# The prompt's attention weighing as three products of high and low parts, in one unit with score and look

## The chip, the cores and the metric

The kernel runs on one core of a Trainium2 chip as a single launch. The metric is device time in microseconds (us), the median of three runs. TensorE (PE in the rows) multiplies matrices, with its weight loads shown apart as PEld; VectorE (DVE), ScalarE (ACT) and GpSimd (POOL) do the elementwise work; SyncE (SP) and GpSimd issue the DMAs. Every engine takes its own instructions strictly in the order in which the program lists them and waits on counters (semaphores) where it needs another engine's result.

## What is computed, cut to what matters

The kernel is one inference step of a two-layer decoder for a prompt of 2048 tokens and for 8 sample sequences of 8 tokens. Layer 0 has eight heads of "FoX" attention (attention with a forget gate), whose prompt part and sample part are the subject here; retention, a gated linear recurrence, projections and norms around it are not touched.

```python
def fox_prompt(q, k, v, logf):                 # per head: 2048 queries, 2048 keys, 64 values wide
    cum = jnp.cumsum(logf, axis=1)
    ...
    s = jnp.einsum('bqhd,bkhd->bhqk', qi, k) * scale
    s = s + ci.transpose(0, 2, 1)[..., None] - cum_t[:, :, None, :]
    s = jnp.where((qpos[:, None] >= kpos[None, :])[None, None], s, NEG_INF)
    p = jax.nn.softmax(s, axis=-1)
    return jnp.einsum('bhqk,bkhd->bqhd', p.astype(v.dtype), v)      # the weighing

def fox_sample(q, k, v, logf, k_past, v_past, logf_past):           # 8 x 8192 cached rows, in pages of 128
    ...
```

All of it is float32.

## The kernel before

The program runs in stages one after the other, each a function with its own loops: input projections, a small preparation, `attention`, `retention`, and the second layer. Only `attention` is touched.

`attention` does two jobs at a time: for head `t` of the prompt the whole causal attention, and for one sample batch the attention over its 64 cached pages (of the next batch the score part, of this batch the weighing part). A loop runs over eight heads, two heads to an iteration, the last two peeled; before it stands an `opening` for the first head's turned inputs and the first batch's scores.

**The prompt's work in one head** is 40 steps. Queries lie in four groups of 512 columns (`G`), keys in tiles of 128, and group `g` needs the key tiles 0 to 4g+3: 4 + 8 + 12 + 16 = 40 steps `s`. The last four tiles of each group are on the diagonal and narrower: 512, 384, 256 and 128 columns. A step has these parts:

- *score* (`score`, L1567 and L1568): two matmuls into one of two PSUM banks `ps_k[s % 2]`. On the diagonal VectorE adds a mask (L1402).
- *exp* (L1288): ScalarE writes `prob[s % 4]`, plain float32.
- *weigh* (L1583): one float32 matmul, stationary `v` with a column of ones (65 columns), moving `prob`, added up in `ps_o`. The program issues one matmul; the trace shows each as two records.
- *look* (L1549, L1550): the scores of a step 18 places ahead (`AHEAD`), turned round, into the one bank `ps_n`; VectorE takes the row maximum (L1383; on the diagonal it first adds a mask, L1379). These give each query's maximum before its scores are made.

A group ends with *keep* (ScalarE copies `ps_o`) and *out* (turned back and normed). During steps 8 to 15 the next head's queries and keys are turned (`turn`): transposes into `ps_x`, ScalarE takes the high part, VectorE the low part, GpSimd a copy (L1242, L1244).

**The samples' work in one head** is 16 rounds of four *page turns* (`s_turn`, L1629: four 128x128 transposes into the one bank `ps_t`, which ScalarE empties for even pages, L1319, and VectorE for odd pages, L1434), a *page score* (L1637, L1641) and a *page weighing* (L1668), and in every other round a *flip* (`s_flip`, L1651: four transposes of sample probabilities into the same bank `ps_t`, emptied by VectorE, L1443; behind it VectorE takes a maximum, L1438). A page turn has to wait until the page before it has been copied out of `ps_t`.

**What sets the order.** `fox_events` lists the prompt's events of a head with a cost each, `samp_events` the samples', and `merge` interleaves the two lists: it takes the next event of whichever list is less far through its total cost, and keeps events of the same kind at least `SPACE` = 0.85 apart where it can. The merged list is walked by every engine: each emits, in that order, its own part of each event. So the list sets TensorE's order and VectorE's and ScalarE's as well. An event of cost 0 is emitted where the merge comes to it, which may be after sample events. Before the change a step gave two events with a cost, score and look together, and the weighing of two steps earlier.

## Time and profile before

| | us |
|---|---|
| median of three runs | 3978.82 (3969.96 to 3981.21) |
| the profiled execution, its own time | 3970.3 |
| its span in the trace | 3968.7 |
| attention's opening (first page turn to the first score) | 925 to 1063 |
| attention's eight heads | 1063 to 2268 |

The page gives TensorE 88% of the span as busy, VectorE 41%, ScalarE 34%, GpSimd 11%. The granted TensorE clock is 0.943 of full speed over the span. The rows further down come from four views: the windows view (busy time of each engine in a stretch, with the granted clock), the lines view (groups of like instructions), the waits view (who waited for whom), and the timeline (instructions in order of time). A timeline row is: start, duration, engine, line, operation, tiles written and read, shapes, how many were merged, and in brackets the idle time before it with what ended it. A matmul's recorded duration runs past the start of the next one, since they are pipelined; what it costs in a stream is the distance from its start to the next start.

### The profile page before, as it was taken

To read this page: it belongs to the slowest core of one execution; us is meant where nothing else is said; L and a number is where in the kernel's file an instruction comes from. 1 tells how busy PE (TensorE), PEld (TensorE's weight loads), DVE (VectorE), ACT (ScalarE), POOL (GpSimd) and SP (SyncE) were. 2 spreads that over 40 slices of the span, in tenths; PEclk is the share of its full clock that TensorE was granted. 3 is DMA by queue.
4 is the path that set the end of the run, shared out by engine and by line. 5 is a ranking of instruction groups with operands and counts; after the bars stand their busy time and mean duration, and the time that the engine had idled before them with its cause. 6 is when DMAs were issued, how large, how long until landed. Compare 5 with 4: busy or idle time off the path is not lost. (4 is left out here: it accounts for less than half of the span.)

```text
span 3968.7 us, 65033 instructions
## 1 busy us (share of the span) xinstructions
PE 3509.9 (88%) x21092; PEld 2631.3 (66%) x21092; DVE 1636.0 (41%) x3074; ACT 1347.8 (34%) x2380; POOL 446.6 (11%) x683
## 2 busy tenths in 40 slices
PE   6999699975799999989999776999968999769998
PEld 5888588863455565555555465788856767558887
DVE  3222311323344454444444255433335676643333
ACT  3111211101233333333333243333335666632322
POOL 0000000101022222222222244000000000000000
PEclk9999899976799999999999988999989999879999
DMA  5223532435577777777776587333234333142221
GB/s 156 108 107 132 170 105 96 141 89 152 152 228 233 224 232 232 236 222 234 231 231 202 153 290 253 130 130 129 105 136 165 126 123 123 58 168 90 90 90 55
DMA packets 381102, 627.46 MB, mean 158 GB/s; under 512 B 124121, under 2 KB 182401, under 8 KB 380802
## 3 DMA queue, kind: packets, MB, share of 16 engines
q1 hardware_dynamic: 339026, 487.55, 37.8%
q0 software_dynamic: 41792, 136.48, 10.8%
q8 instruction: 135, 2.21, 0.2%
q14 instruction: 149, 1.22, 0.1%
HBM read 488.67 MB, written 135.22 MB: 157 GB/s over the span
## 5 line engine op out<-in xcount | busy, mean ns | idle before, releaser
L1629 PEld LDWEIGHTS att_samp_ps_t<-att_ident,att_samp_k_ring 128*128 128x128 f32 x2048 | 238.7, 147 | 283.1 <-issue 233.6
L1629 PE MATMUL att_samp_ps_t<-att_ident,att_samp_k_ring 128*128 128x128 f32 x2048 | 339.7, 291 | 84.9 <-DVE att_samp_kt L1434 43.8
L123 PE MATMUL in_ps_z<-in_w_hi,in_u_hi 128*128 128x512 f32 x952 | 376.3, 395 | 40.8 <-DVE in_w_lo L157 40.8
L1229 POOL DMA_DIRECT2D att_samp_v_ring<-cache_v x512 | 274.9, 537 | 974.4 <-issue 971.1
L124 PE MATMUL in_ps_z<-in_w_lo,in_u_hi 128*128 128x512 f32 x952 | 374.6, 394 | 0.0
L125 PE MATMUL in_ps_z<-in_w_hi,in_u_lo 128*128 128x512 f32 x952 | 374.6, 393 | 0.0
L1319 ACT COPY att_samp_kt<-att_samp_ps_t 128x512 f32<-128x512 f32 x256 | 149.8, 585 | 502.8 <-PE att_samp_ps_t L1629 501.5
L1434 DVE COPY att_samp_kt<-att_samp_ps_t 128x512 f32<-128x512 f32 x256 | 176.2, 688 | 293.6 <-PE att_samp_ps_t L1629 288.5
L1583 PE MATMUL att_fox_ps_o<-att_fox_prob,att_fox_v_one 128*65 128x512 f32 (+3 forms) x640 | 287.7, 533 | 3.8 <-ACT att_fox_prob L1288 3.8
L1383 DVE TENSOR_REDUCE att_fox_part_max<-att_fox_ps_n 128x1 f32<-128x512 f32 (+2 forms) x320 | 195.0, 609 | 123.1 <-PE att_fox_ps_n L1550 112.9
L123 PEld LDWEIGHTS in_ps_z<-in_w_hi,in_u_hi 128*128 128x128 f32 x952 | 181.4, 191 | 80.1 <-issue 28.6
L1288 ACT ACTIVATE att_fox_prob<-att_fox_ps_k 128x512 f32<-128x512 f32 (+1 forms) x320 | 169.9, 536 | 183.5 <-DVE att_fox_ps_k L1402 103.2
L123 PE MATMUL tail_ps_g<-tail_wg_hi,tail_h_hi 128*128 128x512 f32 x544 | 216.1, 397 | 13.2 <-DVE tail_p_lo L2317 9.9
L125 PE MATMUL tail_ps_g<-tail_wg_hi,tail_h_lo 128*128 128x512 f32 x544 | 212.6, 391 | 0.0
L124 PE MATMUL tail_ps_g<-tail_wg_lo,tail_h_hi 128*128 128x512 f32 x544 | 212.5, 391 | 0.0
L125 PEld LDWEIGHTS in_ps_z<-in_w_hi,in_u_lo 128*128 128x128 f32 x952 | 181.3, 190 | 38.3
L124 PEld LDWEIGHTS in_ps_z<-in_w_lo,in_u_hi 128*128 128x128 f32 x952 | 181.5, 191 | 37.3
L1668 PEld LDWEIGHTS att_samp_ps_v<-att_samp_v_ring,att_samp_prob_t 128*32 128x32 f32 x4096 | 115.5, 111 | 82.8 <-issue 69.1
L2345 DVE SCALAR_TENSOR_TENSOR tail_e<-tail_ps_g,tail_e 128x512 f32<-128x512 f32 x68 | 47.0, 691 | 277.9 <-ACT tail_ps_g L2278 277.9
L1567 PE MATMUL att_fox_ps_k<-att_fox_q_a,att_fox_k_a 128*128 128x512 f32 (+1 forms) x320 | 160.4, 501 | 0.0
L1641 PE MATMUL att_samp_ps_s<-att_samp_kt,att_samp_q_diagonal 128*32 128x512 f32 x1024 | 145.7, 643 | 3.5 <-DVE att_samp_kt L1434 3.5
L1668 PE MATMUL att_samp_ps_v<-att_samp_v_ring,att_samp_prob_t 128*32 128x128 f32 x4096 | 137.7, 276 | 10.4 <-DMA att_samp_v_ring<-cache_v 9.9
(376 smaller groups left out, 7006.4 us busy)
## 6 DMA issues: line engine op xcount, KB each, us to landing
att_samp_v_ring<-cache_v POOLq DMA_DIRECT2D x512, 256.0 KB, 3.8
att_samp_k_ring<-cache_k SPq DMA_DIRECT2D x512, 256.0 KB, 3.6
tail_a_hi<-a_hi SPq DMA_DIRECT2D x34, 512.0 KB, 5.7
tail_a_lo<-a_lo SPq DMA_DIRECT2D x34, 512.0 KB, 5.9
in_w_stage<-w_in_even SPq DMA_DIRECT2D x64, 256.0 KB, 6.4
lru_u_hi<-u_hi SPq DMA_DIRECT2D x8, 2048.0 KB, 8.0
lru_u_lo<-u_lo SPq DMA_DIRECT2D x8, 2048.0 KB, 13.1
in_x<-x SPq DMA_DIRECT2D x17, 512.0 KB, 3.8
```

Source lines behind the costliest of these rows:

```text
L123: pe.matmul(out, act_hi, w_hi, start=start, stop=False)
L124: pe.matmul(out, act_hi, w_lo, start=False, stop=False)
L125: return pe.matmul(out, act_lo, w_hi, start=False, stop=stop)
L1229: pool.dma_start(v_ring[:, p, g, :], row(io["cache_v"], page)).then_inc(vp_in[y], 16)
L1288: act.activation(prob[:, s % 4, r:G], ps_k[:, s % 2, r:G], ACT.Exp).then_inc(exped.sem, 1)
L1319: act.copy(kt[:, n % 2, :, p * PAGE:(p + 1) * PAGE], ps_t[:, :].rearrange("p (a k) -> p a k", a=PAIRS)).then_inc(k_even.sem, 1)
L1383: dve.tensor_reduce(part_max[:, g, b % B4, c:c + 1], ps_n[:, 0:w], AX.X, ALU.max).then_inc(maxed.sem, 1)
L1434: dve.tensor_copy(kt[:, n % 2, :, p * PAGE:(p + 1) * PAGE], ps_t[:, :].rearrange("p (a k) -> p a k", a=PAIRS)).then_inc(k_odd.sem, 1)
L1567: pe.matmul(ps_k[:, s % 2, r:G], k_a[:, par, k], q_a[:, par, q], start=True, stop=False)
L1583: pe.matmul(ps_o[0:HD + 1, r:G], v[:, par, kt, :], prob[:, s % 4, r:G], start=kt == 0, stop=kt == B4 * (g + 1) - 1).then_inc(weighed.sem, 1)
L1629: last = pe.transpose(ps_t[:, a * PAGE:(a + 1) * PAGE], k_ring[:, n % 2, p, a * P:(a + 1) * P], ident[:, :])
L1668: last = pe.matmul(ps_v[strip, g, :], prob_t[:, c % 2, at:at + 2 * R], v_ring[:, p, g, a * P:(a + 1) * P], start=c == 0 and p == 0, stop=c ...
```

## The change

The weighing becomes three matmuls in the reduced float32 type (`F32R`) that scores and looks use: values and probabilities are each split into a high part (rounded to `F32R`) and a low part (the rest), and `split3` (unchanged, L119 to L125) adds up high x high, low x high and high x low. For that:

- ScalarE takes the exponential twice from the same score bank, into `p_hi` (`F32R`, 3 buffers) and into `prob` (float32, 2 buffers instead of 4).
- VectorE gets a new event *cut*: `p_lo = prob - p_hi`. The weighing waits for it (`prob_cut`) instead of for the exponential.
- The values of a head are no longer loaded by `fetch` straight into place. A new event *load_v* loads them into the buffer of the turned queries once those are turned (SyncE), and *cut_v* makes `v_hi` (ScalarE) and `v_lo` (VectorE). They are 66 columns wide instead of 65.
- In the merge's list, weighing of step s-2, score of s and look make one event with the summed cost (0.7 + 0.46 + 0.46). The *cut* of step s-1 follows it as an event of cost 0.

```diff
@@ fox_events
-            for s in range(steps + 2):
+            for s in range(steps + LAG):
+                unit, cost = [], 0.0
+                if s >= LAG:
+                    g, kt = group_of(s - LAG)
+                    unit.append(("weigh", g, s - LAG, kt))
+                    cost += 0.7 * cut_width(kt - B4 * g)
                 if s < steps:
                     g, kt = group_of(s)
-                    pair = [("score", g, s, kt)]
-                    cost = 0.46 * cut_width(kt - B4 * g)
+                    unit.append(("score", g, s, kt))
+                    cost += 0.46 * cut_width(kt - B4 * g)
...
-                        pair.append(("look", dt, ng, b, c, n))
+                        unit.append(("look", dt, ng, b, c, n))
                         cost += 0.46
-                    out.append((cost, *pair))
-                if s >= 2:
-                    g, kt = group_of(s - 2)
-                    out.append((0.87 * cut_width(kt - B4 * g), ("weigh", g, s - 2, kt)))
+                out.append((cost, *unit))
+                if 1 <= s <= steps:
+                    out.append((0.0, ("cut", group_of(s - 1)[0], s - 1, group_of(s - 1)[1])))
...
+                    if not last and s == TURN + 2 * GQ + 2:
+                        out.append((0.0, ("load_v", 1)))
+                    if not last and s == TURN + 2 * GQ + 7:
+                        out.append((0.0, ("cut_v", 1)))
@@ sync
-                sp.dma_start(v[:, par, :, 0:HD], io["fv"]...).then_inc(v_in[par], 16)
...
+            def load_v(t, i, par, dt):
+                t, i, par = ahead(t, i, par, dt)
+                sp.wait_ge(*turned.at(t))
+                sp.sem_inc(sp_passed, 1)
+                sp.dma_start(nat[:, 0], io["fv"][0:PT, :, bass.ds(t * HD, HD)]...).then_inc(v_in[par], 16)
@@ scalar
-                act.wait_ge(*(weighed.at(t, s - 4) if s >= 4 else weighed.at(t - 1, s - 4 + steps)))
-                act.activation(prob[:, s % 4, r:G], ps_k[:, s % 2, r:G], ACT.Exp).then_inc(exped.sem, 1)
+                act.wait_ge(*(weighed.at(t, s - 3) if s >= 3 else weighed.at(t - 1, s - 3 + steps)))
+                act.activation(p_hi[:, s % 3, r:G], ps_k[:, s % 2, r:G], ACT.Exp)
+                act.wait_ge(*(prob_cut.at(t, s - 2) if s >= 2 else prob_cut.at(t - 1, s - 2 + steps)))
+                act.activation(prob[:, s % 2, r:G], ps_k[:, s % 2, r:G], ACT.Exp).then_inc(exped.sem, 1)
+
+            def cut_v(t, i, par, dt):
...
+                act.copy(v_hi[:, par, :, 0:HD], nat[:, 0]).then_inc(v_high.sem, 1)
@@ vector
+            def cut(t, i, par, g, s, kt):
+                r = max(kt - B4 * g, 0) * P
+                dve.wait_ge(*exped.at(t, s))
+                dve.wait_ge(*(weighed.at(t, s - 2) if s >= 2 else weighed.at(t - 1, s - 2 + steps)))
+                dve.tensor_tensor(p_lo[:, s % 2, r:G], prob[:, s % 2, r:G], p_hi[:, s % 3, r:G].bitcast(F32), ALU.subtract)\
+                    .then_inc(prob_cut.sem, 1)
+
+            def cut_v(t, i, par, dt):
...
+                dve.tensor_tensor(v_lo[:, par, :, 0:HD], nat[:, 0], v_hi[:, par, :, 0:HD].bitcast(F32), ALU.subtract).then_inc(v_low.sem, 1)
@@ tensor
-                pe.wait_ge(*exped.at(t, s))
+                pe.wait_ge(*prob_cut.at(t, s))
...
-                pe.matmul(ps_o[0:HD + 1, r:G], v[:, par, kt, :], prob[:, s % 4, r:G],
-                          start=kt == 0, stop=kt == B4 * (g + 1) - 1).then_inc(weighed.sem, 1)
+                split3(pe, ps_o[0:HD + 2, r:G], v_hi[:, par, kt, :], v_lo[:, par, kt, :], p_hi[:, s % 3, r:G], p_lo[:, s % 2, r:G],
+                       kt == 0, kt == B4 * (g + 1) - 1).then_inc(weighed.sem, 1)
```

How the order moves is shown at two places of a head. The first is the stretch behind score and look of step 8, where a round's page score and page weighing stand. TensorE before (`ps_n` is the look, `ps_t` a page turn, `ps_s` the page score, `ps_v` the page weighing, `ps_o` the prompt's weighing, `ps_x<-ident,fox_natural` a turn of the next head's inputs):

```order
L1550 MATMUL att_fox_ps_n<-att_fox_k_b,att_fox_q_b 128x512
L1629 MATMUL att_samp_ps_t<-att_ident,att_samp_k_ring 128x128 x4
L1641 MATMUL att_samp_ps_s<-att_samp_kt,att_samp_q_diagonal 32x512 x4
L1663 ISA
L1668 MATMUL att_samp_ps_v<-att_samp_v_ring,att_samp_prob_t 32x128 x16
L1627 REGISTER_ALU
L1629 MATMUL att_samp_ps_t<-att_ident,att_samp_k_ring 128x128 x4
L1583 MATMUL att_fox_ps_o<-att_fox_prob,att_fox_v_one 65x512
L1629 MATMUL att_samp_ps_t<-att_ident,att_samp_k_ring 128x128 x4
```

TensorE after, at the same place:

```order
L1599 MATMUL att_fox_ps_n<-att_fox_k_b,att_fox_q_b 128x512
L1678 MATMUL att_samp_ps_t<-att_ident,att_samp_k_ring 128x128 x4
L1690 MATMUL att_samp_ps_s<-att_samp_kt,att_samp_q_diagonal 32x512 x4
L1712 ISA
L1717 MATMUL att_samp_ps_v<-att_samp_v_ring,att_samp_prob_t 32x128 x16
L1676 REGISTER_ALU
L1678 MATMUL att_samp_ps_t<-att_ident,att_samp_k_ring 128x128 x4
L1644 REGISTER_ALU
L1646 ISA
L1649 MATMUL att_fox_ps_x<-att_ident,att_fox_natural 64x128 x4
L1628 REGISTER_ALU
L123 MATMUL att_fox_ps_o<-att_fox_p_hi,att_fox_v_hi 66x512
```

The weighing no longer parts two page turns; it has moved behind the turn of the next head's inputs, to the front of the next unit. VectorE at this place, before (score mask, look maximum, odd page's copy, low part of the turned inputs):

```order
L1402 TENSOR_TENSOR att_fox_ps_k<-att_fox_ps_k,att_mask_t 128x128
L1377 REGISTER_ALU
L1383 TENSOR_REDUCE att_fox_part_max<-att_fox_ps_n 128x1
L1431 REGISTER_ALU
L1434 COPY att_samp_kt<-att_samp_ps_t 128x4x128
L1420 REGISTER_ALU
L1423 TENSOR_TENSOR att_fox_q_a<-att_fox_ps_x,att_fox_q_a 64x512
```

and after:

```order
L1439 TENSOR_TENSOR att_fox_ps_k<-att_fox_ps_k,att_mask_t 128x128
L1414 REGISTER_ALU
L1420 TENSOR_REDUCE att_fox_part_max<-att_fox_ps_n 128x1
L1480 REGISTER_ALU
L1483 COPY att_samp_kt<-att_samp_ps_t 128x4x128
L1443 REGISTER_ALU
L1445 TENSOR_TENSOR att_fox_p_lo<-att_fox_prob,att_fox_p_hi 128x512
L1469 REGISTER_ALU
L1472 TENSOR_TENSOR att_fox_q_a<-att_fox_ps_x,att_fox_q_a 64x512
```

The cut for the next weighing (`p_lo`) stands behind the look's maximum and behind the copy of the odd page, whose transposes TensorE issues last before that weighing. The second place is a flip, four steps later. VectorE after:

```order
L1420 TENSOR_REDUCE att_fox_part_max<-att_fox_ps_n 128x1
L1490 REGISTER_ALU
L1491 REGISTER_ALU
L1492 COPY att_samp_prob_t<-att_samp_ps_t 128x512
L1487 TENSOR_REDUCE att_samp_tops<-att_samp_scores 128x1
L1443 REGISTER_ALU
L1445 TENSOR_TENSOR att_fox_p_lo<-att_fox_prob,att_fox_p_hi 128x128
```

Here the copy of the flip and the samples' maximum (`tops`) stand ahead of the cut as well; before, the same two were followed by no work that a weighing waits for.

## Rows read from the trace of the kernel before

**Rows 1.** Windows: stretch, each engine's busy us (instructions), granted clock, DMA share, GB/s.
```profile
1227.00:1386.00 159.00, 144.28 (x1259) 90.48 (x1258) 75.86 (x167) 58.81 (x125) 39.73 (x73) 0.99 0.75 232
...
2018.00:2173.50 155.50, 145.29 (x1259) 91.64 (x1259) 75.37 (x165) 57.41 (x119) 39.74 (x73) 0.99 0.71 220
2173.50:2268.00 94.50, 83.30 (x787) 50.71 (x784) 31.36 (x79) 29.37 (x61) 30.05 (x56) 0.98 0.56 162
```

**Rows 2.** Waits, 1060 to 2270: who waited for whom, us in total, times, longest.
```profile
PE att_fox_ps_o L1583 <- ACT att_fox_prob L1288: 3.8, 7, 0.6
```

**Rows 3.** Timeline, 1500 to 1503: TensorE's steps at full width.
```profile
1500.81 1.02 PE L1583 MATMUL att_fox_ps_o<-att_fox_prob,att_fox_v_one 128*65 128x512 f32 x2
...
1501.72 0.66 PE L1629 MATMUL att_samp_ps_t<-att_ident,att_samp_k_ring 128*128 128x128 f32 x4
...
1502.13 0.48 PE L1567 MATMUL att_fox_ps_k<-att_fox_q_a,att_fox_k_a 128*128 128x512 f32 x1
...
1502.45 0.40 PE L1568 MATMUL att_fox_ps_k<-att_fox_q_b,att_fox_k_b 98*128 98x512 f32 x1
...
1502.69 0.40 PE L1549 MATMUL att_fox_ps_n<-att_fox_k_a,att_fox_q_a 128*128 128x512 f32 x1
...
1502.92 0.39 PE L1550 MATMUL att_fox_ps_n<-att_fox_k_b,att_fox_q_b 96*128 96x512 f32 x1
```

**Rows 4.** Timeline, 1503 to 1507: look's maximum; page, page score, page weighing, odd page.
```profile
1503.34 0.63 PE L1629 MATMUL att_samp_ps_t<-att_ident,att_samp_k_ring 128*128 128x128 f32 x4
1503.35 0.69 DVE L1383 TENSOR_REDUCE att_fox_part_max<-att_fox_ps_n 128x1 f32<-128x512 f32 x1 [0.15 <-PE att_fox_ps_n L1550]
...
1503.90 1.07 PE L1641 MATMUL att_samp_ps_s<-att_samp_kt,att_samp_q_diagonal 128*32 128x512 f32 x8
...
1504.78 1.06 PE L1668 MATMUL att_samp_ps_v<-att_samp_v_ring,att_samp_prob_t 128*32 128x128 f32 x32
...
1505.77 0.66 PE L1629 MATMUL att_samp_ps_t<-att_ident,att_samp_k_ring 128*128 128x128 f32 x4
...
...
1506.46 0.69 DVE L1434 COPY att_samp_kt<-att_samp_ps_t 128x512 f32<-128x512 f32 x1 [2.42 <-PE att_samp_ps_t L1629]
```

**Rows 5.** Timeline, 1508 to 1511: an odd page right behind a masked look.
```profile
1508.61 0.65 PE L1629 MATMUL att_samp_ps_t<-att_ident,att_samp_k_ring 128*128 128x128 f32 x4
1508.78 0.30 DVE L1379 TENSOR_TENSOR att_fox_ps_n<-att_fox_ps_n,att_mask 128x128 f32<-128x128 f32 x1 [1.63 <-PE att_fox_ps_n L1550]
...
1509.12 0.56 DVE L1383 TENSOR_REDUCE att_fox_part_max<-att_fox_ps_n 128x1 f32<-128x384 f32 x1
1509.59 0.68 DVE L1434 COPY att_samp_kt<-att_samp_ps_t 128x512 f32<-128x512 f32 x1
...
1510.42 0.63 PE L1629 MATMUL att_samp_ps_t<-att_ident,att_samp_k_ring 128*128 128x128 f32 x4 [0.30 <-DVE att_samp_kt L1434]
```

**Rows 6.** Lines, 1060 to 2270: busy us, mean ns of one.
```profile
L1438 DVE TENSOR_REDUCE att_samp_tops<-att_samp_scores 128x1 f32<-128x512 f32 x58 | 39.3, 677 | 3.2 <-ACT att_samp_scores L1325 2.2 <-DVE att_fox_q_a L1423 0.6
...
L1288 ACT ACTIVATE att_fox_prob<-att_fox_ps_k 128x512 f32<-128x512 f32 x224 | 134.4, 601 | 90.8 <-PE att_fox_ps_k L1568 80.1 <-DVE att_fox_ps_k L1402 10.6
...
L1244 POOL CAST att_fox_k_a<-att_fox_k_a 64x512 fp32r<-64x512 f32 x28 | 17.1, 609 | 17.3 <-ACT att_fox_k_a L1299 15.9 <-issue 0.9 <-POOL att_fox_q_b L1242 0.2
```

**Rows 7.** One line's instructions: duration in ns, min/median/max; high-low split elsewhere.
```profile
L157 DVE TENSOR_TENSOR in_w_lo<-in_w_stage,in_w_hi x56: 681/692/695, 17.1 to 484.2; 128x512 fp32r<-128x512 f32 x56
```

**Rows 8.** Timeline: the end of a head on TensorE.
```profile
1382.12 0.43 PE L1590 MATMUL att_fox_ps_x<-att_ident,att_fox_o_t 65*128 65x65 f32 x4 [1.57 <-ACT att_fox_o_t L1293]
1385.88 0.47 PE L1629 MATMUL att_samp_ps_t<-att_ident,att_samp_k_ring 128*128 128x128 f32 x1 [3.32 <-issue]
```

**Rows 9.** Windows in which TensorE is less busy: granted clock behind POOL's busy time.
```profile
1382.00:1390.00 8.00, 4.11 (x16) 3.11 (x16) 1.93 (x6) 3.07 (x11) 0.00 (x0) 0.57 0.71 143
...
970.00:985.00 15.00, 10.31 (x67) 5.77 (x65) 7.44 (x16) 3.51 (x6) 0.00 (x0) 1.00 0.51 167
1015.00:1060.00 45.00, 32.41 (x135) 15.23 (x135) 8.10 (x12) 8.19 (x14) 0.00 (x0) 0.61 0.43 133
```

More of the change, by code:

```diff
@@ L963, in attention @@
         AHEAD = 18
+        LAG = 2
         TURN = 8
@@ L1058, in attention @@
         weighed = ph.count("weighed", steps, 4)
+        prob_cut = ph.count("prob_cut", steps, 4)
+        sp_passed = ph.sem("sp_passed")
+        v_high = ph.count("v_high")
+        v_low = ph.count("v_low")
         o_copied = ph.count("o_copied", GQ)
@@ L1195, in s_score @@
                     load_bias(b + 1, n // 2 + 2 - NVC)
-            one, step = run({"s_turn": s_turn, "s_score": s_score})
+            def load_v(t, i, par, dt):
+                t, i, par = ahead(t, i, par, dt)
+                sp.wait_ge(*turned.at(t))
+                sp.sem_inc(sp_passed, 1)
+                sp.dma_start(nat[:, 0], io["fv"][0:PT, :, bass.ds(t * HD, HD)].rearrange("t p d -> p t d")).then_inc(v_in[par], 16)
+            one, step = run({"load_v": load_v, "s_turn": s_turn, "s_score": s_score})
             one(-1, -1, 1, opening)
             sp.wait_ge(*turned.at(0))
+            sp.wait_ge(*v_low.at(0))
             fetch(1, 1)
@@ L1348, in s_share @@
                 act.activation(share[:, :], moved[:, :, 0], ACT.Exp, bias=least[:, :], scale=-1.0).then_inc(shared.sem, 1)
-            one, step = run({"top": top_keep, "exp": exps, "keep": copy_out, "turn": turn, "s_place": s_place, "s_turn": s_turn,
+            one, step = run({"top": top_keep, "exp": exps, "cut_v": cut_v, "keep": copy_out, "turn": turn, "s_place": s_place, "s_turn": s_turn,
                              "s_keep": s_keep, "s_exp": s_exp, "s_exp_new": s_exp_new, "s_share": s_share})
@@ L1510, in s_rows @@
                     .then_inc(out_kept.sem, 1)
-            one, step = run({"look": look, "make_top": make_top, "score": mask_score, "out": norm, "turn": turn, "s_turn": s_turn, "s_top": s_top,
+            one, step = run({"look": look, "cut": cut, "cut_v": cut_v, "make_top": make_top, "score": mask_score, "out": norm, "turn": turn, "s_turn": s_turn, "s_top": s_top,
                              "s_flip": s_flip, "s_bias_new": s_bias_new, "s_negate": s_negate, "s_flip_new": s_flip_new, "s_total": s_total,
```

28 lines of the change are left out of this document (21 added, 7 removed).

## The prediction

> **What bounds the kernel now.** Read the windows first [rows 1]. From 1227 to 2173.5 lie six equal heads, so one takes 157.8 us, and TensorE is busy for 144 to 146 us of it at a granted clock of 0.99. VectorE is busy for 75 and ScalarE for 57 to 59. So TensorE is the bound of the heads, and the weighing, which the change shortens, lies on it. Then the waits [rows 2]: today's weighing hardly ever waits for its exponential, 3.8 us in all. That is what the change touches, since it puts one more engine between exponential and weighing. Last the timeline [rows 3 to 5], which shows what each step costs in the stream and how long VectorE needs from a look, or from a page, until TensorE can go on. The waits of the six heads are short but many; which wait ends last has to be read step by step.
>
> **What the change saves on TensorE.** A full weighing starts at 1500.81 and the page behind it at 1501.72: 0.91 us. A matmul of the reduced type costs 0.24 from start to start (1502.45 to 1502.69, 1502.69 to 1502.92) [rows 3]; I take 0.23, and three are 0.69. Gain 0.22. Of 320 weighings 224 are full, and they give 49 us. The narrower ones I put at zero: the new cost there has three matmuls' fixed parts in it and the old one is plainly proportional to columns. The price of 0.23 comes from matmuls with 128 stationary columns; with 66 there is no reason in the rows for another.
>
> **What it adds off TensorE.** A second exponential per step, 0.60 [rows 6], on ScalarE; a subtraction with two operands in SBUF per step on VectorE, 0.69 for 512 columns by a like one elsewhere [rows 7]; per head a copy and a subtraction of 1024 columns, twice that row at most. VectorE goes from 75 to about 100 us per head and ScalarE from 58 to about 80, so neither becomes the bound by its load. The load of the values moves in SyncE's queue behind the turn of the queries, which lies three steps back by then; behind it queue the page loads, and I cost that at nothing, since there is nothing left to wait for. If it did wait, page turns would wait too.
>
> **What it adds as a chain.** TensorE's order of one step is now weigh, score, look as one unit, then sample work, then the next unit, which begins with a weighing. That weighing needs its cut; VectorE does the cut behind the maximum of the look that TensorE has just issued, and, where the merge has put a page's or a flip's copy ahead of it, behind that too. TensorE stands at the weighing, with score, look and every later page queued behind it. I count from the point at which TensorE could start its next work after a look, 0.24 after the start of the look's second matmul, and price how late the weighing starts. I went through the 38 units of a head in the order, four cases:
>
> - A, cut right behind the look's maximum (12 units). From 1502.92 + 0.24 = 1503.16: the maximum runs to 1504.04 [rows 4], the cut 0.69 more, and some 0.15 pass from VectorE's end to TensorE's start (1510.27 to 1510.42) [rows 5]: 1.72 after the point. A masked look adds up to 0.3, so 1.8 each, 22 us. TensorE has one or two pages to do there, which fit inside.
> - B, an odd page or a flip between. In rows 5 the point is the page's start, 1508.61; mask, maximum and page copy end at 1510.27, 1.66 later; cut and hand-over add 0.84: 2.5. Four such with an odd page, two of them lengthened by work on the next head's inputs: 11 us. Seven flips, six with the samples' maximum (0.68, [rows 6]) ahead of the cut as well: 3.1 each, 22 us.
> - C, page, page score, page weighing, odd page, then the cut (9 units). In rows 4 that odd page starts 2.6 after the point (1505.77) and its copy ends at 1507.15, 4.0 after; the cut 0.69 and 0.15: 4.8, 43 us. Today the weighing starts 0.5 after that page's start.
> - D, cut early, but an odd page and then a whole round follow (4 units). The second page waits for the copy of the first, 1.8 (1508.61 to 1510.42, [rows 5]); the round from page to odd page adds 2.4 (1503.34 to 1505.77, [rows 4]) and that page 0.4: 4.6 each, 18 us.
>
> The last two units of a head, with the samples' closing arithmetic on VectorE, I put at 10 us. That makes 126 us between units. The units: 0.69 + 0.56 (score: 0.32 + 0.24) + 0.47 (look) = 1.72 at full width [rows 3], 60 us for the 38, the narrower ones scaled by their columns. The first two steps of a head take 4, and its end 2 (two weighings and the wait of 1.57 for the last copy, [rows 8]). Sum: 192 us, against 157.8: **34 us more per head**, and 239 for seven. The eighth head has no page turns: its 20 units with a look cost 1.7 + 1.8, and the 18 without, where only exponentials (1.2), cut and hand-overs lie between a score and its weighing two units on, about 1.8 each; with start and end 108 against 94.5 [rows 1], 14 more. Together 253 us with TensorE's clock as it is now.
>
> **The clock.** The sum has TensorE idle for some 68 of 192 us per head, in pieces of one to two and a half us. What the clock does then is shown only elsewhere. Around the waits at a head's end, 1.57 and 3.32 [rows 8], the granted clock is 0.57 over 8 us, so partly at the lower of the two levels (1.2 GHz against 2.4). From 1015 to 1060 TensorE is busy for 72% and is granted 0.61; from 970 to 985 it is busy for 69% and is granted 1.00 [rows 9]. The new heads would be busy for about 70%, in the same region, with denser work than those stretches. I take a mean of 0.9, nearer the full clock because every round still holds a long unbroken run. TensorE's work is then 124 us a head and some 80 in the last, 950 us in all; at 0.9 it takes 106 more.
>
> Sum: 253 + 106 = 359 us on the profiled execution's 3970.3, so 4329. The median of the runs lies 8.5 above that execution, so **4335 us**, 9% more.
>
> **A rule on the shared port.** The heads' VectorE instructions of today that I priced read PSUM or one SBUF tensor, so no row shows the cut beside GpSimd's casts of 0.61 [rows 6], eight a head. The Trainium skill, SBUF — State Buffer, section "SBUF: two separate sides", says that a VectorE operation with two SBUF inputs and a GpSimd operation that reads SBUF lock each other out for the whole instruction, whoever starts first. No run here shows it yet. By that rule each cast could hold up a cut by its whole length: by an estimate from the row, at most 8 x 0.61 x 8 = 39 us more; by the rows alone, nothing. I leave it out of the sum.
>
> **Rivals.** (1) *Chain, but no loss of clock*: the pieces of idle time are too short to matter, as from 970 to 985. 3979 + 253 = 4232. (2) *Chain, and a deeper loss*: at a mean of 0.75 TensorE's 950 us take 317 more: 4549. The rows from 1015 to 1060 speak for it, the denser work against. (3) *Chain half hidden*: VectorE takes the cuts earlier than I think, or today's head holds waits that go away; 17 a head, 3979 + 126 = 4105, and in the mildest form no change. (4) *Faster*: the cut is off TensorE's path. This is decided behind a look: if the cut ended before the pages that stand there (0.4 to 0.7 in A, 2.9 in C), the weighing would start as today and only the 49 us would count, 3930. For it speaks that today's weighing waits for nothing [rows 2]; against it, that the chain of 1.7 or more begins with the look itself, and its parts are rows of their own: the maximum in rows 4, the cut in rows 7, the hand-over in rows 5. (5) *The three products don't run at 0.23* with 66 stationary columns but at twice that: 0.69 x 224 = 155 more, about 4490. Nothing in the rows speaks for it.
>
> **How the numbers follow.** Forecast 0.43; rival (1) 0.22; (2) 0.13; (3) 0.11, a third of it without change; (4) 0.08; (5) 0.03. A measurement of this kernel tells 0.3%, about 12 us, from no change. So faster 0.08, the same 0.04, slower 0.88. The range goes from 4110 (chain mostly half hidden) to 4530 (clock at about 0.76 with the chain); below it are (4) and most of (3), above it half of (2).
>
> **What would show it.** In the profile after, the first of the weighing's three matmuls (line 123, `att_fox_ps_o`) should be the costliest waiter on TensorE, ended by VectorE's `att_fox_p_lo`, with some 300 us over the phase where 3.8 stand now; a full weighing should cost 0.69 from start to start; heads should last 190 to 210 us; page turns' own waits should fall. Granted clock in the heads should be 0.85 to 0.95. A head of 157 us or less, or a weighing that still waits for nothing, would make the prediction wrong at the chain; a head of 192 with the clock at 0.99 would make it wrong at the clock alone.

## The result, and the profile after

The changed kernel takes **4253.6 us** (median of 4 runs, 4249.6 to 4262.8) beside 3975.4 of the kernel before: ratio 1.0716, 95% interval 1.0699 to 1.0733 (the two medians alone give 1.0700). It is 278 us slower. The profiled execution has a span of 4251.3 us, 282.6 above that of before (3968.7). TensorE's first work of each head shows where they lie: the heads now begin at 1059.0, 1254.6, 1448.5, 1639.9, 1834.2, 2025.6, 2216.1 and 2408.1, and the last ends at 2543.3. Seven heads took 1110.3 us and take 1349.1, so 238.8 more; the last took 94.5 and takes 135.2, 40.7 more; the opening is 4 shorter, and what follows the attention 7 longer.

First the windows of one middle head, of its last microseconds, and of the last head in two pieces (columns as in [rows 1]).

```profile
1448.50:1639.90 191.40, 146.79 (x1300) 102.77 (x1301) 98.10 (x204) 75.03 (x157) 40.80 (x73) 0.95 0.63 190
1624.00:1634.60 10.60, 7.91 (x84) 4.73 (x82) 5.77 (x15) 2.68 (x8) 3.75 (x7) 1.00 0.77 265
1634.60:1648.30 13.70, 9.21 (x46) 7.49 (x50) 6.74 (x20) 6.13 (x19) 0.00 (x0) 0.50 0.63 139
1648.30:1743.80 95.50, 72.69 (x660) 51.19 (x652) 51.77 (x106) 38.67 (x83) 23.11 (x40) 1.00 0.62 186
2408.10:2491.00 82.90, 60.37 (x644) 43.48 (x647) 28.37 (x62) 21.85 (x51) 30.04 (x56) 0.79 0.64 185
2491.00:2543.30 52.30, 36.59 (x185) 21.91 (x185) 24.70 (x58) 24.32 (x51) 0.00 (x0) 0.96 0.00 1
```

The head lasts 191.4 us and TensorE is busy for 146.8 of them; before, it was 144 to 146 of 157.8. VectorE and ScalarE have risen to 98 and 75 (forecast about 100 and 80) and bound nothing by their load. The granted clock is 0.95: full for most of a head, and at the lower level around its end. In the last head no engine but these three works behind 2491: the sample work is used up there.

Then TensorE's waits over the eight heads (who waited for whom, us in total, times, longest), which answer to [rows 2]. First those of the page turns in the kernel before:

```profile
PE att_samp_ps_t L1629 <- DVE att_samp_kt L1434: 26.4, 35, 1.9
PE att_samp_ps_t L1629 <- ACT att_samp_kt L1319: 6.6, 9, 2.5
PE att_samp_ps_t L1629 <- DVE att_samp_prob_t L1443: 4.6, 15, 0.4
```

and in the changed kernel:

```profile
PE att_fox_ps_o L123 <- DVE att_fox_p_lo L1445: 194.4, 179, 3.3
PE att_samp_ps_t L1678 <- ACT att_samp_kt L1355: 45.4, 64, 2.5
PE att_samp_ps_t L1678 <- DVE att_samp_kt L1483: 29.7, 29, 1.3
PE att_samp_ps_t L1678 <- DVE att_samp_prob_t L1492: 28.1, 28, 1.2
PE att_samp_ps_v L1717 <- DMA att_samp_v_ring<-cache_v: 19.6, 9, 3.5
```

The 3.8 us of before have become 194 us in which the weighing waits for the cut. But page turns wait, too, 103 us over these heads where it was 38, and the experiments show that this is a cost of its own.

Two stretches of the timeline, to be held against [rows 4, 5]. First one of case C, a look with page, page score, page weighing and odd page behind it:

```profile
1710.68 0.61 ACT L1316 ACTIVATE att_fox_prob<-att_fox_ps_k 128x512 f32<-128x512 f32 x1
...
1712.18 0.34 PE L1599 MATMUL att_fox_ps_n<-att_fox_k_b,att_fox_q_b 96*128 96x384 f32 x1
1712.36 0.60 PE L1678 MATMUL att_samp_ps_t<-att_ident,att_samp_k_ring 128*128 128x128 f32 x4
...
1712.89 0.56 DVE L1420 TENSOR_REDUCE att_fox_part_max<-att_fox_ps_n 128x1 f32<-128x384 f32 x1
...
1715.19 0.66 PE L1678 MATMUL att_samp_ps_t<-att_ident,att_samp_k_ring 128*128 128x128 f32 x4
1715.88 0.69 DVE L1483 COPY att_samp_kt<-att_samp_ps_t 128x512 f32<-128x512 f32 x1 [2.44 <-PE att_samp_ps_t L1678]
1716.49 0.68 DVE L1445 TENSOR_TENSOR att_fox_p_lo<-att_fox_prob,att_fox_p_hi 128x512 fp32r<-128x512 f32 x1
...
1717.23 0.45 PE L123 MATMUL att_fox_ps_o<-att_fox_p_hi,att_fox_v_hi 128*66 128x512 f32 x1 [1.38 <-DVE att_fox_p_lo L1445]
```

VectorE stands idle for 2.44 us ahead of the page's copy, with the next cut behind that copy; the cut's own input, the exponential in the first row, was ready at 1711.29, 5.2 us before the cut began. The weighing starts 2.0 us after the page and waits 1.38 for the cut. Now case A, with two pages behind the look:

```profile
1708.83 0.40 PE L1599 MATMUL att_fox_ps_n<-att_fox_k_b,att_fox_q_b 96*128 96x512 f32 x1
...
1709.07 0.60 PE L1678 MATMUL att_samp_ps_t<-att_ident,att_samp_k_ring 128*128 128x128 f32 x4
1709.27 0.69 DVE L1420 TENSOR_REDUCE att_fox_part_max<-att_fox_ps_n 128x1 f32<-128x512 f32 x1 [0.33 <-PE att_fox_ps_n L1599]
...
1709.71 0.58 ACT L1355 COPY att_samp_kt<-att_samp_ps_t 128x512 f32<-128x512 f32 x1 [1.49 <-PE att_samp_ps_t L1678]
1709.88 0.68 DVE L1445 TENSOR_TENSOR att_fox_p_lo<-att_fox_prob,att_fox_p_hi 128x512 fp32r<-128x512 f32 x1
1709.90 1.13 POOL L1270 CAST att_fox_k_a<-att_fox_k_a 64x512 fp32r<-64x512 f32 x1
...
1710.35 0.66 PE L1678 MATMUL att_samp_ps_t<-att_ident,att_samp_k_ring 128*128 128x128 f32 x4 [0.68 <-ACT att_samp_kt L1355]
...
1710.76 0.48 PE L123 MATMUL att_fox_ps_o<-att_fox_p_hi,att_fox_v_hi 128*66 128x512 f32 x1
```

Maximum, cut and hand-over end where I had put them, 1.69 us after 1709.07. Yet the weighing waits for nothing: the second page started only at 1710.35, since it writes the PSUM bank of the first and had to wait 0.68 for that one's copy. Two causes end here at the same time, and only a run without the cut can tell which of them sets it.

### The profile page after: what moved, and what is told of

Read it like the earlier page. It is cut to its first block and busy times, and to the rows that moved or that the text cites. A ratio compares the mean times of both kernels' runs of the same rounds, so it can differ in the third digit from the quotient of the medians.

```text
span 4251.3 us, 67158 instructions
## 1 busy us (share of the span) xinstructions
PE 3530.4 (83%) x21412; PEld 2722.3 (64%) x21412; DVE 1822.4 (43%) x3403; ACT 1495.5 (35%) x2708; POOL 452.6 (11%) x683
## 5 line engine op out<-in xcount | busy, mean ns | idle before, releaser
L1678 PEld LDWEIGHTS att_samp_ps_t<-att_ident,att_samp_k_ring 128*128 128x128 f32 x2048 | 248.3, 149 | 251.8 <-issue 179.0
L125 PE MATMUL in_ps_z<-in_w_hi,in_u_lo 128*128 128x512 f32 x952 | 372.9, 392 | 0.0
L123 PE MATMUL att_fox_ps_o<-att_fox_p_hi,att_fox_v_hi 128*66 128x512 f32 (+1 forms) x320 | 139.4, 436 | 200.4 <-DVE att_fox_p_lo L1445 194.4
L1314 ACT ACTIVATE att_fox_p_hi<-att_fox_ps_k 128x512 fp32r<-128x512 f32 (+1 forms) x320 | 171.5, 536 | 299.2 <-PE att_fox_ps_k L1617 163.0
L123 PEld LDWEIGHTS att_fox_ps_o<-att_fox_p_hi,att_fox_v_hi 128*66 128x66 f32 x320 | 45.5, 142 | 268.6 <-DVE att_fox_p_lo L1445 255.1
L125 PE MATMUL tail_ps_g<-tail_wg_hi,tail_h_lo 128*128 128x512 f32 x544 | 213.3, 392 | 0.0
L125 PEld LDWEIGHTS in_ps_z<-in_w_hi,in_u_lo 128*128 128x128 f32 x952 | 180.3, 189 | 38.1
L1445 DVE TENSOR_TENSOR att_fox_p_lo<-att_fox_prob,att_fox_p_hi 128x512 fp32r<-128x512 f32 (+1 forms) x320 | 192.2, 603 | 12.7 <-ACT att_fox_prob L1316 11.0
```

What stands on the lines that cost most here:

```text
L123: pe.matmul(out, act_hi, w_hi, start=start, stop=False)
L125: return pe.matmul(out, act_lo, w_hi, start=False, stop=stop)
L1314: act.activation(p_hi[:, s % 3, r:G], ps_k[:, s % 2, r:G], ACT.Exp)
L1445: dve.tensor_tensor(p_lo[:, s % 2, r:G], prob[:, s % 2, r:G], p_hi[:, s % 3, r:G].bitcast(F32), ALU.subtract)\
L1678: last = pe.transpose(ps_t[:, a * PAGE:(a + 1) * PAGE], k_ring[:, n % 2, p, a * P:(a + 1) * P], ident[:, :])
```

## The experiments

The theory at the start was the chain through VectorE; the rival, that the unit itself costs the time; a third, that the new arithmetic does, whatever the order. Medians are beside the kernel before on the same chip (3970 to 3975), each ratio with its 95% interval. "Late" is, as in the prediction, the start of a weighing after the point 0.24 behind the start of the look's second matmul, a mean over six heads.

**The cut ahead of the maximum.** TensorE's order is untouched.

```diff
                 unit, cost = [], 0.0
+                if 1 <= s <= steps:
+                    unit.append(("cut", group_of(s - 1)[0], s - 1, group_of(s - 1)[1]))
                 if s >= LAG:
...
                 out.append((cost, *unit))
-                if 1 <= s <= steps:
-                    out.append((0.0, ("cut", group_of(s - 1)[0], s - 1, group_of(s - 1)[1])))
```

> The changed kernel with one event moved: the cut of step s-1 stands ahead of the unit of step s, so on VectorE ahead of the look's maximum and of the page and flip copies behind it; TensorE's own order is the same. Theory (chain look, maximum, cut, weighing): the waits of the weighing for the low part, 194 us in the changed kernel, fall below 30; heads fall from 192 to about 160; 3990 us, between 3930 and 4060. Rival (the unit itself costs it, since weighing, score and look now crowd TensorE's pages together): heads stay above 180 and the time above 4150. Granted clock in the heads by the theory back from 0.95 to 0.98 or more.

4053.4 us, 1.0215 (1.0195 to 1.0235). 200 of the 278 us are gone, and heads last 165.6, so the place of the cut on VectorE is the main cause. The granted clock of the six middle heads is back at 0.98, and what that gives is part of the 200. 78 us over the 3975 of before stay, where I had expected 15, and the waits of this run say where (over the heads):

```profile
PE att_samp_ps_t L1678 <- ACT att_samp_kt L1355: 45.4, 64, 2.3
PE att_samp_ps_t L1678 <- DVE att_samp_kt L1483: 38.3, 35, 1.4
PE att_fox_ps_o L123 <- DVE att_fox_p_lo L1445: 34.9, 48, 2.3
PE att_samp_ps_t L1678 <- DVE att_samp_prob_t L1492: 29.3, 35, 1.2
```

The weighing's wait has fallen from 194 to 35; those of the page turns have not fallen at all.

**The order alone.** The kernel before, with its fp32 weighing, in the unit. The planner counts that weighing at its old 0.87, so a full unit is worth 1.79 and not 1.62, and the merged order is not quite that of the changed kernel.

```diff
-                    pair = [("score", g, s, kt)]
...
-                if s >= 2:
-                    g, kt = group_of(s - 2)
-                    out.append((0.87 * cut_width(kt - B4 * g), ("weigh", g, s - 2, kt)))
+                pair, cost = [], 0.0
+                if s >= 2:
+                    g, kt = group_of(s - 2)
+                    pair.append(("weigh", g, s - 2, kt))
+                    cost += 0.87 * cut_width(kt - B4 * g)
+                if s < steps:
+                    pair.append(("score", g, s, kt))
```

> The kernel before with the unit alone: weighing, score and look of one step as one event, the weighing still one fp32 product of one exponential, no cut. Theory: no chain through VectorE, so the weighing waits for nothing; what the unit costs is the page turns that crowd behind it, at most the 66 us by which waits of page turns rose in the changed kernel: 4010 us, between 3975 and 4045. Rival (the unit is the cause): 4150 to 4250.

4047.4 us, 1.0201 (1.0180 to 1.0221): 77 us, 2 above the top of what I expected. There is no cut in this kernel; heads last 166.2 us (8.4 more) and the last one 115.6 (21 more). What has risen is the waits of the page turns, from 38 to 117 us over the heads:

```profile
PE att_samp_ps_t L1633 <- DVE att_samp_kt L1438: 44.3, 42, 1.2
PE att_samp_ps_t L1633 <- ACT att_samp_kt L1323: 37.0, 51, 2.5
PE att_samp_ps_t L1633 <- DVE att_samp_prob_t L1447: 35.7, 35, 1.2
```

So the unit has a price of its own, though not that of the rival.

**The unit without the cut.** The changed kernel with one exponential, no cut, and the high part twice, so that TensorE does the same matmuls; the low part of the probabilities is left out of the result.

```diff
                 act.activation(p_hi[:, s % 3, r:G], ps_k[:, s % 2, r:G], ACT.Exp)
-                act.wait_ge(*(prob_cut.at(t, s - 2) if s >= 2 else prob_cut.at(t - 1, s - 2 + steps)))
-                act.activation(prob[:, s % 2, r:G], ps_k[:, s % 2, r:G], ACT.Exp).then_inc(exped.sem, 1)
...
-                pe.wait_ge(*prob_cut.at(t, s))
+                pe.wait_ge(*exped.at(t, s))
...
-    p_hi[:, s % 3, r:G], p_lo[:, s % 2, r:G],
+    p_hi[:, s % 3, r:G], p_hi[:, s % 3, r:G],
```

> The changed kernel in its own order without the second exponential and without the cut; the product with the low part uses the high part again, so TensorE does the same three matmuls. Theory: what is left of the change is the unit, 77 us in the run of the order alone, less what three products save where the weighing stands in one piece with score and look: 0.91 to 0.75, 36 us at most: 4020 us, between 4005 and 4045. So the second exponential and the cut cost some 235 us in the changed kernel, of which 200 come from the place of the cut on VectorE (4254 less 4053). Rival (TensorE saves nothing there either): 4045 to 4055.

4010.6 us, 1.0108 (1.0085 to 1.0132). That is 37 less than the order alone. So the 278 us can be told as steps between measured runs: the unit +77, the three products, with the order that their price in the planner gives, -37, second exponential and cut +43 where the cut stands ahead of the maximum, and its place behind maximum and copies +200. (The steps join neighbouring runs, so that they add up, to 283, proves nothing by itself; the 5 over 278 are the difference between two medians of the kernel before.) TensorE's order is the same in the three kernels of the next table. One unit of each kind, late in us:

| behind the look | changed kernel | cut ahead | no cut |
|---|---|---|---|
| A: page, page | 1.70 | 1.70 | 1.70 |
| B: flip, then a turn of tops | 2.43 | 0.75 | 0.69 |
| C: page, score, weighing, odd page | 4.86 | 3.23 | 3.24 |
| D: odd page, then a whole round | 4.52 | 4.47 | 4.47 |
| all 38 of a head | 120.1 | 95.2 | 92.4 |

B and C wait for the cut. A and D are as late without any cut: there the second page waits for the bank of the first. And of the 120.1 us of a head 92.4 stay without the cut: sample work that TensorE does there in any case, and waits of pages.

**The cut made longer.** A maximum of the same columns ahead of each cut, which nobody reads.

```diff
+                dve.tensor_reduce(spare[:, s % 4:s % 4 + 1], prob[:, s % 2, r:G], AX.X, ALU.max)
                 dve.tensor_tensor(p_lo[:, s % 2, r:G], prob[:, s % 2, r:G], p_hi[:, s % 3, r:G].bitcast(F32), ALU.subtract)\
```

> The changed kernel with one more VectorE instruction ahead of every cut, a maximum over the same columns of the exponential that nobody reads (about 0.6 us at full width). Theory: in 34 of 38 units of a head, and in most of the last head, the cut ends TensorE's wait, so the addition is paid almost whole: some 19 us a head and 10 in the last, about 145 in all, 4400 us (4360 to 4430). Rival (something else is late there and the cut only seems last): below 4300.

4472.6 us, 1.1266 (1.1236 to 1.1296): 219 more than the changed kernel, and not 145. The sign and the place are as expected:

```profile
PE att_fox_ps_o L123 <- DVE att_fox_p_lo L1447: 299.3, 228, 3.3
```

The size is not. The units are later by 23.2 us a head, where I had reckoned 19; but the heads grew by 29.5, and their granted clock fell from 0.95 to 0.87. I take the rest for the clock's price, which is not shown: no run isolates it.

**The weighing apart.** The changed kernel, but the weighing is an event of its own behind score and look, as before, at the planner's new price of 0.70.

```diff
-                if s >= LAG:
-                    g, kt = group_of(s - LAG)
-                    unit.append(("weigh", g, s - LAG, kt))
-                    cost += 0.7 * cut_width(kt - B4 * g)
...
+                if s >= LAG:
+                    g, kt = group_of(s - LAG)
+                    out.append((0.7 * cut_width(kt - B4 * g), ("weigh", g, s - LAG, kt)))
```

> The changed kernel with the weighing as an event of its own behind score and look, as in the kernel before; the cut stays behind the look's maximum. Theory: score and look of the step, and often a page, lie between the maximum that VectorE does ahead of the cut and the weighing that needs it, so the wait is covered: waits for the low part below 40 us, heads about 160, 3985 us, between 3920 and 4080. Rival (three products and their second exponential and cut are too much for the engines, whatever the order): above 4150.

3971.5 us, 1.0006 (0.9994 to 1.0017). The weighing waits 8.5 us for its cut, and the whole loss is gone with the cuts still behind the maxima. So the third theory falls: the arithmetic is not too much for the engines. But neither does the saving on TensorE show, and the next runs ask why.

**Exactly the order of before.** The same with the planner's old price of 0.87, by which every old event stands where it stood; then with the cut ahead of the maximum too; then without second exponential and cut (the low part left out as above).

```diff
-                    out.append((0.7 * cut_width(kt - B4 * g), ("weigh", g, s - LAG, kt)))
+                    out.append((0.87 * cut_width(kt - B4 * g), ("weigh", g, s - LAG, kt)))
```

> The three products in exactly the order of the kernel before on every engine: the weighing apart, behind score and look, and weighed in the planner with the old price of 0.87; the cuts stay behind the looks' maxima. Theory: TensorE saves about 0.16 us at each full weighing (0.91 before, 0.75 in the changed kernel), some 36 us, and page turns give part of it back, since their copies queue behind exponentials and cuts (their waits rose by 42 us with the weighing apart and the new price): 3960 us, between 3935 and 3975. Rival (the time given back came from the other merge, by the new price): 3925 to 3935.

```diff
+                if 1 <= s <= steps:
+                    out.append((0.0, ("cut", group_of(s - 1)[0], s - 1, group_of(s - 1)[1])))
                 if s < steps:
                     g, kt = group_of(s)
                     unit.append(("score", g, s, kt))
...
                 out.append((cost, *unit))
-                if 1 <= s <= steps:
-                    out.append((0.0, ("cut", group_of(s - 1)[0], s - 1, group_of(s - 1)[1])))
```

> The same with the cut ahead of the look's maximum on VectorE. Theory: with the weighing apart its cut was not late any more, so its place matters only for the copies behind it: within 10 us of the run with the cut behind the maximum. Rival (a chain through the maximum is still paid with the weighing apart): 20 us or more faster than that run.

```diff
-                act.activation(prob[:, s % 2, r:G], ps_k[:, s % 2, r:G], ACT.Exp).then_inc(exped.sem, 1)
...
-                pe.wait_ge(*prob_cut.at(t, s))
+                pe.wait_ge(*exped.at(t, s))
```

> The three products in the order of the kernel before, but without the second exponential and without the cut; the product with the low part uses the high part again, so TensorE does the same three matmuls. Theory: what page turns gave back came from ScalarE and VectorE, so the whole saving of TensorE shows: 3930 us, between 3920 and 3942, and the waits of page turns are back at the 65 us of the kernel before. Rival (three short matmuls save nothing beside the page turns, which are bound by the round trip of their bank anyway): 3955 or more, with page waits above 90 us.

4026.6 (1.0130, 1.0105 to 1.0154), 4108.3 (1.0340, 1.0312 to 1.0367) and 3977.5 (1.0011, 1.0000 to 1.0022): three misses. Without any new work on VectorE and ScalarE, three short matmuls in the old place save nothing. That is the time which the rival named there; its other mark, page turns that wait for more than 90 us, is missed: from 900 on they wait 82 us, where it was 65 before. Second exponential and cut cost 49 us in this order. And a cut ahead of the maximum, which gave 200 us in the unit, costs 82 in this order. What VectorE waited for ahead of its cuts (us, times), first with the cut behind the maximum, then ahead of it:

```profile
  ACT att_fox_prob L1316: 11.7, 7
```

```profile
  ACT att_fox_prob L1316: 141.1, 88
```

In this order the exponential isn't there yet when VectorE reaches the early cut, and the copy of an odd page stands behind it; TensorE's wait for those copies rose from 65 to 114 us (from 900 on), 49 of the 82.

**One product only.** As the run without the cut in the old order, with the first of the three matmuls alone; both products with low parts are left out.

```diff
-                split3(pe, ps_o[0:HD + 2, r:G], v_hi[:, par, kt, :], v_lo[:, par, kt, :], p_hi[:, s % 3, r:G], p_hi[:, s % 3, r:G],
-                       kt == 0, kt == B4 * (g + 1) - 1).then_inc(weighed.sem, 1)
+                pe.matmul(ps_o[0:HD + 2, r:G], v_hi[:, par, kt, :], p_hi[:, s % 3, r:G],
+                          start=kt == 0, stop=kt == B4 * (g + 1) - 1).then_inc(weighed.sem, 1)
```

> The order of the kernel before, one exponential, no cut, and of the three products of the weighing only the first: the two with the low parts are left out, so the output lacks them. Against the run with three matmuls and no cut TensorE does 0.46 us less at each of 224 full weighings, 103 us and a little more at the narrow ones. Theory: 16 of 28 full weighings of a head stand between two page turns, and the step from page to page lasts 1.36 (after an even page) or 1.58 us (after an odd one) whether the weighing between takes 0.95 or 0.75, since both pages use one PSUM bank; so there a shorter weighing gives nothing, and at most the other 12 a head, 40 us in all, show: 3940 us, between 3925 and 3965, with the step from page to page over a weighing still 1.36 and 1.58. Rival (the three products are as dear as the fp32 one in the stream, and the pages only seem to bind): 3870 to 3890.

3956.1 us, 0.9961 (0.9945 to 0.9976): 103 us less work, 21 us less time. The same page, weighing and page in the kernel before, with three matmuls and with one:

```profile
1565.47 0.60 PE L1629 MATMUL att_samp_ps_t<-att_ident,att_samp_k_ring 128*128 128x128 f32 x4
1565.91 1.02 PE L1583 MATMUL att_fox_ps_o<-att_fox_prob,att_fox_v_one 128*65 128x512 f32 x2
1566.82 0.44 PE L1629 MATMUL att_samp_ps_t<-att_ident,att_samp_k_ring 128*128 128x128 f32 x2
```

```profile
1564.06 0.60 PE L1672 MATMUL att_samp_ps_t<-att_ident,att_samp_k_ring 128*128 128x128 f32 x4
...
1564.77 0.59 ACT L1352 COPY att_samp_kt<-att_samp_ps_t 128x512 f32<-128x512 f32 x1 [0.87 <-PE att_samp_ps_t L1672]
1564.96 0.39 PE L125 MATMUL att_fox_ps_o<-att_fox_p_hi,att_fox_v_lo 128*66 128x512 f32 x1
...
1565.41 0.44 PE L1672 MATMUL att_samp_ps_t<-att_ident,att_samp_k_ring 128*128 128x128 f32 x2
```

```profile
1558.88 0.60 PE L1672 MATMUL att_samp_ps_t<-att_ident,att_samp_k_ring 128*128 128x128 f32 x4
...
1560.23 0.44 PE L1672 MATMUL att_samp_ps_t<-att_ident,att_samp_k_ring 128*128 128x128 f32 x2 [0.52 <-ACT att_samp_kt L1352]
```

From page to page it is 1.35 us in all three. Over six heads the medians of this step, with a full weighing between, are 1.361, 1.361 and 1.359 after an even page (30 cases) and 1.587, 1.583 and 1.582 after an odd one (54). Both pages use one bank, and its round trip, transposes, hand-over, copy and hand-over, lasts that long. After an even page the fp32 weighing of the kernel before fills it all but to the end: no wait is seen, and next to nothing can be saved.

**The price in the planner.** The kernel before with one number changed; the weighing apart at 0.80; and the weighing apart at 0.70 without second exponential and cut (low part left out).

```diff
-                    out.append((0.87 * cut_width(kt - B4 * g), ("weigh", g, s - 2, kt)))
+                    out.append((0.70 * cut_width(kt - B4 * g), ("weigh", g, s - 2, kt)))
```

> The kernel before with one number of the planner changed: a weighing is reckoned at 0.70 and not at 0.87, which gives the order that the run with the weighing apart had, with weighing, score and look mostly together between two pages. Theory: in that order the weighing isn't hidden between two pages any more and fp32 costs its full 0.91, so against the three products in this order (3972) the fp32 weighing loses some 30 us in TensorE and gains some 50 for the exponentials and cuts that it doesn't need: 3955 us, between 3925 and 3990. Rival (the new order is simply worse, and three products repair it): 4000 or more.

```diff
-                    out.append((0.7 * cut_width(kt - B4 * g), ("weigh", g, s - LAG, kt)))
+                    out.append((0.80 * cut_width(kt - B4 * g), ("weigh", g, s - LAG, kt)))
```

> The run with the weighing apart, its price in the planner 0.80 and not 0.70. Theory: the order has the same patterns between pages (18 times weighing, score and look together, 17 at 0.70; 2 against 20 weighings alone at 0.87), so the time stays near that run: 3975 us, between 3955 and 4000. Rival (the time goes smoothly with the price, from 3972 at 0.70 to 4027 at 0.87): 4000 to 4010.

```diff
-                act.activation(prob[:, s % 2, r:G], ps_k[:, s % 2, r:G], ACT.Exp).then_inc(exped.sem, 1)
...
-                pe.wait_ge(*prob_cut.at(t, s))
+                pe.wait_ge(*exped.at(t, s))
```

> The run with the weighing apart at the price of 0.70, without the second exponential and without the cut, with three matmuls as above. Theory: in this order weighing, score and look stand together between pages, so the products' saving shows against the fp32 weighing in the same order (3975): some 30 us, 3945 us, between 3935 and 3960, and the exponentials and cuts of the run with the weighing apart (3972) cost what the products save. Rival (the page turns bind in this order too): 3968 or more.

3974.7 (1.0008, 0.9998 to 1.0017), 3994.7 (1.0056, 1.0037 to 1.0074) and 3952.2 (0.9961, 0.9941 to 0.9982). At 0.70 weighing, score and look stand mostly together between two pages. There the fp32 weighing is no worse off than in the old order, three products save 22 us, and the exponentials and cuts take 19 back. TensorE's order is the same in the kernels at 0.70, and no page stands behind most of their weighings, so here the weighing's own price can be read, as the time from its start to the look that follows weighing and score. With fp32:

```profile
1450.71 1.02 PE L1583 MATMUL att_fox_ps_o<-att_fox_prob,att_fox_v_one 128*65 128x512 f32 x2
...
1452.03 0.40 PE L1549 MATMUL att_fox_ps_n<-att_fox_k_a,att_fox_q_a 128*128 128x512 f32 x1
```

and with three products:

```profile
1440.56 0.47 PE L123 MATMUL att_fox_ps_o<-att_fox_p_hi,att_fox_v_hi 128*66 128x512 f32 x1
...
1441.80 0.40 PE L1592 MATMUL att_fox_ps_n<-att_fox_k_a,att_fox_q_a 128*128 128x512 f32 x1
```

That is 1.32 against 1.24 us, and the medians of 82 such places are the same. So three products save 0.08 at a full weighing, 18 us for 224 by an estimate from these rows, close to the 22 measured. Both new prices lie below the 0.85 that the merge wants between two looks, the old one above, and so the orders differ in kind. The run at 0.80 came out between 0.70 and 0.87, nearer to the rival than to what I expected; why it is 23 us slower than at 0.70 stays open. None of the runs that compute the whole result is faster than the kernel before.

## Why the prediction was right, and where it wasn't

The range held the time, and the sign is clear; but the forecast is 81 us too high, and the first rival (chain, and no loss of clock, 4232) came nearer. (Two slips of the working: 4329 and 8.5 make 4338, not 4335; and 68 idle of 192 is busy for 65%, not about 70%.)

- **The chain, 239 us for seven heads.** Measured 238.8. That it fits so well is partly luck, since two errors cancel: the total of the late starts was put at 126 us a head and is 120.1; units with start and end at 66 and are 72. TensorE's waits for the cut are 194 us, where I had said some 300; the rest of the late starts was there without it. B (2.5 to 3.1) measured 2.1 to 3.2, C (4.8) 4.4 to 4.9 and once, behind a group's end, 5.5, D (4.6) 4.3 to 4.5, and A (1.8) 1.6 to 1.9 where two pages stand.
- **The cause of A was wrong.** I wrote that TensorE's one or two pages "fit inside" maximum and cut. With two pages the second waits for the bank of the first, and the weighing is as late without a cut. The price agrees because both chains happen to end together. That the unit crowds page turns was in my numbers for A and D, never as a term of its own: it costs 77 us, and the forecast credited all but D's part to the cut. I even wrote that the page turns' own waits should fall; they rose from 38 to 103.
- **The saving on TensorE, 49 us.** I read 0.91 us from start to start of weighing and next page and took it for the weighing's price. That stretch is also the rest of a bank's round trip. The saving is 0 in the old order and 22 us at the price of 0.70; the 37 in the unit come with another order, and how much of them is the products' stays open. Two sizes were wrong. A full weighing of the kernel before is worth 0.86 (in the kernel before at 0.70 a turn of maxima follows the weighing of 1481.49, and starts 0.86 behind it), not 0.91. And it now takes 0.75 to 0.78, not 0.69: the first of its matmuls has 0.29 to 0.31 to the next, the others 0.23. So the gain is 0.08 to 0.11 and not 0.22.
- **The last head, 14 us.** Measured 40.7. The term was mis-sized at one place: I took its samples to be spread as before. The merge puts off an event with a look until other work worth 0.85 has been placed; the weighing at 0.87 used to be that work, and in the unit only samples are left for it. So by the eighteenth unit they are used up (the window from 2491 on), and the page weighings stand so close that they wait for their loads: 19.6 us, where it was 9.9. The order alone has 21 of these us; the rest came with the new arithmetic, where TensorE waits 16.5 us for the cut and the clock is lower.
- **The clock, 106 us.** The step that failed. I took a mean of 0.9 for all heads; it is 0.94 to 0.96 in the first seven, with 10 to 17 us at the lower level around a head's end and 3.4 in its middle (1743.8 to 1747.2, granted 0.51), and 0.85 in the last. Even at 0.95 my working would ask for 50 us, since it takes TensorE's work to be what everything waits for all the time. Pieces of idle time of one to two us inside the head mostly leave it at the full clock (1648 to 1744: busy for 76%, granted 1.00). What the loss at the heads' ends costs isn't separated. By an estimate from the row of 1634.6, its 9.2 us of busy time would be 4.6 at the full clock: at most some 5 us a head, 32 for seven. The 6 us a head by which units, start and end came out dearer are the room for it, and dearer weighings (28 times 0.06) take 1.7 of them.
- **The second exponential, and the loads of VectorE and ScalarE.** As forecast, 0.60 a step, and neither engine is a bound by its load. They still cost 43 us in the unit with the cut ahead, 49 in the old order and 19 with the weighing apart, which I had at nothing beside the chain. In the unit it is the weighing's wait for its cut (34.9) and not the page turns (113 us with, 111 without); apart, it is 8.5 of that wait and 8 of page turns.
- **The shared port.** The lock is there, but of the estimate of at most 39 us nothing is seen on the path: see the last section.

## What to carry to other kernels

Work that stands between two uses of one buffer is free as long as it is shorter than the buffer's round trip; before making it faster, measure the step from use to use, and not that of the work. Binding steps into a unit takes from the planner the pieces with which it covered such round trips, and it puts whatever one of them waits for ahead of all the others. Of a new step on a second engine ask what stands ahead of it in that engine's order: here the cut and its exponential cost 43 us, the maximum and the copies in front of it 200, and the same move that repaired this in one order was a loss in the other.

## What the runs showed of the hardware

GpSimd's casts had one length before, and have another beside the cuts (min, median and max in ns; before, then after):

```profile
L1244 POOL CAST att_fox_k_a<-att_fox_k_a x32: 607/609/611, 930.4 to 2081.4; 64x512 fp32r<-64x512 f32 x32
```

```profile
L1270 POOL CAST att_fox_k_a<-att_fox_k_a x32: 607/609/1139, 925.9 to 2285.9; 64x512 fp32r<-64x512 f32 x32
```

In the timeline of case A the cast of 1.13 us begins 0.02 after a cut of 0.68, and its end is that cut's end and 0.47 more. Of the 56 casts in the heads 20 overlap a cut, and of those that don't none is longer than 0.62. In 19 of the 20 the cut began first, and each of these casts ends 0.47 us behind the cut, however long the two overlap; in the last one the cast was first, and the cut took 0.87. In the run with the cut ahead of the maximum a cast is first more often, and there it is the cut that grows, to at most 1.07:

```profile
L1445 DVE TENSOR_TENSOR att_fox_p_lo<-att_fox_prob,att_fox_p_hi x320: 279/681/1072, 1067.4 to 2345.2; 128x512 fp32r<-128x512 f32 x128, 128x256 fp32r<-128x256 f32 x32
```

The Trainium skill, SBUF — State Buffer, section "SBUF: two separate sides", says that these two kinds of operation block each other for the whole instruction, the first one winning. The trace agrees that the one that comes later waits for the end of the first; of the cast's own 0.61 us, 0.47 are left behind that end, so that 0.14 of it were not held up. In the changed kernel the casts pay nearly all of it, some 6 us in all (20.7 and 19.6 us for 28 casts each, at 0.61 before 34.1 together), and TensorE waits for a cast once, 0.6 us, as it did before.
